# Half of the output-weight split moved behind attention, and the expert-pair sums moved from TensorE to GpSimd, in a one-core decoder layer

## What is computed

```
mix = concat(attn, pool, memo) @ w_o
h1  = layer_norm(alpha * x + mix)
f   = sum over the row's 2 experts e of gate_e * (silu(h1 @ w_gate[e]) * (h1 @ w_up[e])) @ w_down[e]
y   = layer_norm(alpha * h1 + f)
```

## Time and profile before

| | |
|---|---|
| median of 3 runs | 989.77 us (986.93 to 989.87) |
| the profiled execution | 986.13 us, span 984.3 us |
| PE busy | 898.5 us (91%) |
| DVE, ACT, POOL busy | 566.0, 388.0, 237.9 us |
| projections, attention | until about 213 us, until about 447 us |
| output projection and routing | from 450.7 us to about 596 us |
| experts | until about 937 us |
| tail | until 984.3 us |

### The profile page before, as it was taken

The page is one execution under the profiler, slowest core; times in us unless marked ns, Lnnn a source line. Parts: engine busy times, 40 slices in busy tenths (PEclk is TensorE's granted clock), DMA queues, the critical chain, the costliest instruction groups (busy, mean ns, idle before and its releaser), DMA issues.

```text
span 984.3 us, 13505 instructions
## 1 busy us (share of the span) xinstructions
PE 898.5 (91%) x5170; PEld 644.5 (65%) x5170; DVE 566.0 (58%) x1098; ACT 388.0 (39%) x741; POOL 237.9 (24%) x142
## 2 busy tenths in 40 slices
PE   6999999988999999868999986999999999999934
PEld 6999878964555544546878855666666666666511
DVE  6202021037665665574677684677787877777438
ACT  5202010014555655473110032454646464555226
POOL 0000000088100000051000003146555555555200
PEclk9999999998999999998999995999999999999968
DMA  9999999289876856606755536799999999997276
GB/s 354 311 345 369 350 362 369 83 328 259 299 291 245 296 172 234 206 37 263 247 183 212 194 130 214 259 346 362 362 352 362 348 361 368 363 370 283 83 293 252
DMA packets 54849, 273.50 MB, mean 278 GB/s; under 512 B 13984, under 2 KB 16544, under 8 KB 39680
## 3 DMA queue, kind: packets, MB, share of 16 engines
q1 hardware_dynamic: 46016, 247.97, 69.8%
q0 software_dynamic: 8768, 24.66, 7.1%
HBM read 256.33 MB, written 95.30 MB: 357 GB/s over the span
## 4 chain that ended last, share of the span: by engine, by line
PE 76%; DVE 14%; ACT 4%; issue 4%; DMA 2%; SPq 0%; DVEq 0%; POOLq 0%; ACTq 0%
PE psum L680 67%; PE psum L739 4%; PE psum L956 3%; ACT back L1065 1%; DVE stats L1387 1%; DVE back L1397 1%; DVE back L1393 1%; DVE back L1262 1%; DVE back L1384 1%; ACT back L512 1%; DMA middle<-pair_d 1%; PE psum L880 1%; DVE front L1270 1%; DVE front L1272 1%; DVE back L1238 1%
## 5 line engine op out<-in xcount | busy, mean ns | idle before, releaser
L1712 POOL DMA_INDIRECT pair_d<-front,back x32 | 134.4, 4199 | 161.4 <-DVE front L1515 155.6
L680 PE MATMUL psum<-back,front 128*64 128x128 f32 (+1 forms) x904 | 151.8, 361 | 5.5 <-ACT back L512 4.6
L680 PEld LDWEIGHTS psum<-back,front 128*64 128x64 f32 (+1 forms) x904 | 71.3, 148 | 61.4 <-issue 52.3
L680 PE MATMUL psum<-gu_high,xg_high 128*112 128x512 f32 x256 | 104.5, 408 | 2.1 <-DVE xg_low L1500 2.1
L680 PE MATMUL psum<-gu_high,xg_low 128*112 128x512 f32 x256 | 101.8, 398 | 0.0
L680 PE MATMUL psum<-gu_low,xg_high 128*112 128x512 f32 x256 | 101.7, 397 | 0.0
L680 PE MATMUL psum<-x_high,w_high 128*128 128x352 f32 x288 | 94.1, 327 | 8.3 <-DVE w_low L377 8.3
L680 PE MATMUL psum<-x_low,w_high 128*128 128x352 f32 x288 | 93.4, 324 | 0.0
L680 PE MATMUL psum<-x_high,w_low 128*128 128x352 f32 x288 | 93.2, 324 | 0.0
L1515 DVE SCALAR_TENSOR_TENSOR front<-psum,back 112x512 f32<-112x512 f32 x64 | 45.1, 747 | 68.8 <-PE psum L680 68.8
L680 PE MATMUL psum<-front 64*128 64x256 f32 (+5 forms) x320 | 79.9, 521 | 4.0 <-DVE stats L1238 2.7
(11 more groups left out here) (213 smaller groups left out, 1710.9 us busy)
## 6 DMA issues: line engine op xcount, KB each, us to landing
back<-w_gu SPq DMA_DIRECT2D x32, 1024.0 KB, 13.8
out_win_k_s<-cache_win_k SPq DMA_DIRECT2D x16, 2044.0 KB, 13.3
out_win_v_s<-cache_win_v SPq DMA_DIRECT2D x16, 2044.0 KB, 12.6
back<-w_down SPq DMA_DIRECT2D x25, 1024.0 KB, 13.0
front<-w_gu SPq DMA_DIRECT2D x16, 1024.0 KB, 13.0
middle<-w_gu SPq DMA_DIRECT2D x16, 1024.0 KB
back<-winkT SPq DMA_DIRECT2D x8, 1792.0 KB, 7.7
back<-cache_win_v SPq DMA_DIRECT2D x8, 1024.0 KB, 7.5
```

Source lines behind the costliest of these rows:

```text
L680: return nc.tensor.matmul(out, lhsT, rhs, start=start, stop=stop, skip_group_check=True)
L1712: G.indirect_dma_start(pair_d, bass.IndirectOffsetOnAxis(ap=IDX[0:CAP, NE + e:NE + e + 1], axis=0), YS[e % 2][0:CAP, :], None, bounds_chec ...
```

## The change

The split of the output weights keeps tiles 0 to 3 beside attention, now in units 40, 42, 44 and 46, with their low parts on GpSimd. Tiles 4 to 7 are split after attention: ACT's order is then `cat_high` of chunk 0, `wo_high` 4 to 7, `cat_high` of chunks 1 to 3; DVE's order is `cat_low` of chunk 0, `wo_low` 4 to 7, `cat_low` of chunks 1 to 3. PE waits at tiles 4 to 7 for a new semaphore `s_wor`. In the tail PE does nothing more: DVE sums chunks 0 and 1, both ahead of its first normalisation, and GpSimd sums chunks 2 to 8 in place in SBUF. The reads of all nine sums are now from SBUF.

```diff
-        OWN_SUM = (0, 1, 4, 8)
-        PE_SUM = [c for c in range(CH) if c not in OWN_SUM]
+        DVE_SUM = 2
         def row_sum(c):
-            if c in OWN_SUM:
-                return YP[c][:, 0, :]
-            j = PE_SUM.index(c)
-            return PS[:, 1024 * (j % 4):1024 * (j % 4) + 1024]
+            return YP[c][:, 0, :]
         def summed(eng, c):
-            if c in PE_SUM:
-                eng.wait_ge(s_ysum, PE_SUM.index(c) + 1)
+            if c < DVE_SUM:
+                eng.wait_ge(s_vsum, c + 1)
             else:
-                eng.wait_ge(s_vsum, OWN_SUM.index(c) + 1)
+                eng.wait_ge(s_ysum, c - DVE_SUM + 1)
...
-        WO_SPLIT_AT = {40: (0,), 41: (1,), 42: (2,), 43: (3,), 44: (4,), 45: (5,), 46: (6,), 47: (7,)}
+        WO_SPLIT_AT = {40: 0, 42: 1, 44: 2, 46: 3}
+        WO_EARLY = len(WO_SPLIT_AT)
...
# TensorE, the first chunk's products, and its sums in the tail
-                        pe.wait_ge(s_wol, k + 1)
+                        if k < WO_EARLY:
+                            pe.wait_ge(s_wol, k + 1)
+                        else:
+                            pe.wait_ge(s_wor, k - WO_EARLY + 1)
...
-            for j, c in enumerate(PE_SUM):
-                m = rows(c)
-                pe.wait_ge(s_yp[c], 16)
-                if j >= 4:
-                    pe.wait_ge(s_f1, PE_SUM[j - 4] + 1)
-                for n in range(2):
-                    o = row_sum(c)[0:m, 512 * n:512 * n + 512]
-                    mm(o, ident[0:m, 0:m], YP[c][0:m, 0, 512 * n:512 * n + 512], True, False)
-                    last = mm(o, ident[0:m, 0:m], YP[c][0:m, 1, 512 * n:512 * n + 512], False, True)
-                last.then_inc(s_ysum, 1)
...
# ScalarE, after the last unit
-            for c in range(4):
+            cat_rounded(0)
+            for k in range(WO_EARLY, KT):
+                wo_rounded(k)
+            for c in range(1, 4):
                 cat_rounded(c)
...
# VectorE, after the last unit
-            for c in range(4):
+            cat_rest(0)
+            for k in range(WO_EARLY, KT):
+                full, high, low = wo_parts(k)
+                dve.wait_ge(s_hi, len(splits) + 1 + k + 1)
+                V_.tensor_tensor(low, full, high.bitcast(F32), ALU.subtract).then_inc(s_wor, 1)
+            for c in range(1, 4):
                 cat_rest(c)
...
# VectorE, tail
-            own_sum(0)
+            for c in range(DVE_SUM):
+                own_sum(c)
             for c in range(CH):
-                if c + 1 in OWN_SUM:
-                    own_sum(c + 1)
                 normalised(c)
...
# GpSimd
-            for k in range(KT):
+            for k in range(WO_EARLY):
                 full, high, low = wo_parts(k)
...
+            for c in range(DVE_SUM, CH):
+                pool.wait_ge(s_yp[c], 16)
+                y = YP[c][0:rows(c)]
+                G.tensor_tensor(y[:, 0, :], y[:, 0, :], y[:, 1, :], ALU.add).then_inc(s_ysum, 1)
```

More of the change, by code:

```diff
@@ L248, in build @@
         s_xp, s_xe, s_sexp, s_smin, s_srd = sem("s_xp"), sem("s_xe"), sem("s_sexp"), sem("s_smin"), sem("s_srd")
-        s_dve, s_pl, s_qb, s_wol = (sem(n) for n in ("s_dve", "s_pl", "s_qb", "s_wol"))
+        s_dve, s_pl, s_qb, s_wol, s_wor = (sem(n) for n in ("s_dve", "s_pl", "s_qb", "s_wol", "s_wor"))
         s_wo = [sem(f"s_wo{i}") for i in range(2)]
@@ L1026, in _ @@
                 pe.nop()
-            pe.wait_ge(s_yd, 2 * NE)
-            for j, c in enumerate(PE_SUM):
-                m = rows(c)
-                pe.wait_ge(s_yp[c], 16)
-                if j >= 4:
-                    pe.wait_ge(s_f1, PE_SUM[j - 4] + 1)
-                for n in range(2):
-                    o = row_sum(c)[0:m, 512 * n:512 * n + 512]
-                    mm(o, ident[0:m, 0:m], YP[c][0:m, 0, 512 * n:512 * n + 512], True, False)
-                    last = mm(o, ident[0:m, 0:m], YP[c][0:m, 1, 512 * n:512 * n + 512], False, True)
-                last.then_inc(s_ysum, 1)
         @block.scalar
@@ L1085, in o_out, with wo_rounded @@
                 nc.scalar.copy(CAT[:, hp + (0 if kind == "w" else 6), i * P:i * P + P], bank(6 + u % 2)[:, 0:P]).then_inc(s_OB, 1)
+            def wo_rounded(k):
+                act.wait_ge(s_wo[k // 4], 16)
+                full, high, _ = wo_parts(k)
+                nc.scalar.copy(high, full).then_inc(s_hi, 1)
             exps(0, 0)
@@ L1103, in _ @@
                     x_act(e)
-                for k in WO_SPLIT_AT.get(u, ()):
-                    act.wait_ge(s_wo[k // 4], 16)
+                if u in WO_SPLIT_AT:
                     act.wait_ge(s_S, 2 * 32)
                     act.wait_ge(s_store, 16 * (6 + 2 * DB))
-                    full, high, _ = wo_parts(k)
-                    nc.scalar.copy(high, full).then_inc(s_hi, 1)
+                    wo_rounded(WO_SPLIT_AT[u])
             o_out(NU - 1)
@@ L1370, in cat_rest @@
                 full, high, low = cat_parts(c)
-                dve.wait_ge(s_hi, len(splits) + KT + c + 1)
+                dve.wait_ge(s_hi, len(splits) + (KT if c else WO_EARLY) + c + 1)
                 V_.tensor_tensor(low, full, high.bitcast(F32), ALU.subtract).then_inc(s_lo, 1)
-            for c in range(4):
+            cat_rest(0)
[4 more added lines that the diff above has]
+            for c in range(1, 4):
                 cat_rest(c)
```

## The result

| | before | after |
|---|---|---|
| median of 11 runs each | 988.71 us (985.93 to 989.87) | 990.88 us (990.43 to 993.24) |
| ratio of the runs | | 1.0031, 95% interval 1.002 to 1.0042 |
| the profiled execution, its span | 986.13, 984.3 us | 992.58, 990.8 us |
| PE, DVE, POOL busy | 898.5, 566.0, 237.9 us | 878.5, 581.0, 250.8 us |

Slower by 0.31%, 3.1 us by the ratio (the two medians are 2.2 us apart). The forecast was slower by 7.3 us, to 997.1, and its range began at 991.0.

A forecast was written before the change was run, and what follows sets the result against it. The prediction took DVE to bound the tail and the PE, DVE, PE chain the projection's start. -1.6 (weights) + 8.9 (sums) = +7.3 us on the median 989.77 gave 997.1, range 991 to 1000.5.

The forecast's parts named there:

- What bounds the tail, and what the change does to it: Tail: DVE bounds it at 2.72 us a chunk; GpSimd's seven sums and DVE's long instructions take turns, 8.9 us later.
- Rival 1: Tail: no turns, `scalar_tensor_tensor` doesn't wait for GpSimd, DVE ends at 976.4; 7.1 us faster, 982.7; chance 0.12.
- Rival 2: Tail: turns at half the price, t near 1.1 us; +0.6 us in all, 990.4; chance 0.06.
- The price of a turn: Tail: one GpSimd sum adds t = 2.2 us to DVE, seven of them 15.2 us of blocking.
- The tail that it was set against: Tail before: DVE ends at 981.93 and idles 3.60 us, because PE's sum of chunk 2 is late.
- The weight split: Start of the projection: PE's first product 1.6 us earlier (0.22 + 0.28 + 1.08), bounds 0.3 to 2.2 us.
- 0.22 us counted for attention: Attention: removed GpSimd instructions had slowed the divisions on DVE at 442.60, 0.84 against 0.62 us.
- three tiles take 3.3 us: Projection: PE's time for three weight tiles before tile 4, each further one 0.7 us, so it never waits.
- rival 3: Projection: PE waits for the late weight tiles, at most 4.8 us less the gain, 1001; chance 0.04.
- Rivals 3 and 4: Fourth rival, projection: the weight edit does nothing, the copy's chain sets the end; +8.9 - 0.3, 998.4, within the forecast's 0.78.
- The level: Whole kernel: the change of +7.3 us was put on the median of the runs, 989.77, giving 997.1.
- Rival 5: Start of the projection: the fall of PE's granted clock may come elsewhere; 1 us either way, within the forecast's 0.78.

The follow-up runs named there:

- e4: The changed kernel with DVE making all nine sums, one ahead of each normalisation, and GpSimd none: median 986.88 us, ratio 0.9995 to the kernel before.
- e6: The kernel of e1 with GpSimd also making the sums of chunks 2, 3, 5, 6 and 7, unread, into free SBUF: one run, span 986.4 us.
- e1: Only the weight split of the change, with the tail of the kernel before: median 985.87 us, ratio 0.9983 to the kernel before.
- e8: The kernel of e1 with only two weight tiles split beside attention, in units 44 and 46, and six behind it: median 983.96 us, ratio 0.9963.
- e3: The changed kernel unaltered, run again on the chip of e1: median 993.17 us, ratio 1.0057 to the kernel before.
- e2: Only the sums of the change, with the weight split of the kernel before: median 995.76 us, ratio 1.0077 to the kernel before.
- e9: The changed kernel unaltered, run once more on the chip of e11: median 992.95 us, ratio 1.0052 to the kernel before.
- e7: The kernel of e1 with 15 products of constants on PE between the last expert and its first sum: median 983.17 us, ratio 0.9952.
- e10: The kernel of e1 with GpSimd making one sum, chunk 2's, and PE those of 3, 5, 6 and 7: median 984.88 us, ratio 0.997.
- e5: The changed kernel with GpSimd doubling the first row in place instead of adding the second, one SBUF input: one run, span 981.7 us.
- e11: e7 and e8 together, two weight tiles beside attention and PE kept at work before the tail: median 984.13 us, ratio 0.9946.

## Why the prediction came out as it did

**What bounds the tail, and what the change does to it: right.** Seven DVE instructions, no more, were held, one by each GpSimd sum, in turn; ACT had its part ready each time; five chunks at 2.72 us followed. e4 and e6 leave no other cause: without GpSimd 1.28 us, with one operand in PSUM 1.28 us. The Trainium skill's rule (SBUF — State Buffer, § Who interferes with whom) held for `scalar_tensor_tensor`, which no row of before could show. Rivals 1 and 2 are out by the same rows. Rival 2's time, 990.4, is near the first measurement, but its price of 1.1 us a turn isn't what the rows show. Its sum is also 0.8 us too high: it adds the turns to 976.4, which holds idle time that turns would fill, and not to 951.1 + 24.5 = 975.6.

**The price of a turn: mis-sized, and this is the step that failed.** I took t = 2.2 us for what one GpSimd sum adds to DVE, from a single row in which DVE's instruction arrived when GpSimd's had been running for 1.1 us. Such a row shows how early the hold ends, 0.13 us before the record's end, but not how late it begins. In the full turns a held instruction is 3.18 to 3.25 us instead of 1.28, so t is 1.93. The hold ends 0.19 us before the sum does and begins about 0.15 us late, and the small rest is the reciprocal and the gap between instructions, which pass while the sum runs. Seven turns are 13.5 us, where the forecast had 15.2: 1.7 us too much. It is the whole difference between the 8.9 us forecast for the tail and the 7.2 in the pair of profiles. I had a lower bound of 1.65 for t, so the term was in its range, but I centred on the row's upper reading.

**The tail that it was set against: up to 1.1 us off, not settled.** I took DVE's 3.60 us of idle time for a constant. It hangs on PE's clock: in e1 and e8, whose tail is the same code, it was 4.76 and 4.94 us and the time from the last scatter to the end 47.5 us against 46.4 in the profile of before. With seven turns that time is 53.6 to 53.7 us, in all three profiles of the changed kernel. So by the profiles the loss is 6.1 to 7.2 us, and not 8.9. The medians speak for the upper end: e3 is 7.3 us above e1 on the same chip, and e2 is 7.6 us slower than before, each with 2 us or so of uncertainty.

**The weight split: right.** 1.6 us earlier was forecast, e1 measured 1.7 (0.5 to 2.9). `cat_low` at 1.22 us, no wait at tiles 4 to 7 and the gap (1.33 us shorter, where 0.28 + 1.08 = 1.36 had been worked out) all came. The 0.22 us counted for attention can't be told: from the first cast to PE's last attention product the new split takes 20.0 to 20.8 us and the old one 20.4 and 21.0. A slip in the working did no harm: "three tiles take 3.3 us" is the time of eight products, and nine take 3.56. Rivals 3 and 4 are out for this split; e8 shows rival 3 in small, 0.3 us, with six late tiles. That the casts of the even units are the costly ones was right too: taking out two of them brought 2.0 us. The forecast said that this cost stays, which is why the edit brought so little.

**The level: 1.1 us off.** I put the change on the median of three runs, 989.77. Eleven gave 988.71. Rival 5, the clock, is real but goes with the execution and not with the edit: chunk 0's 48 products took 12.7 to 13.8 us in the profiles in which PE didn't wait for a tile, 12.74 before and 12.91 after.

Together: 7.3 less 1.7 (turns) and up to 1.1 (tail) is 4.5 to 5.6 us. The repeats measured 5.6 and 5.1 (1.0057 and 1.0052), and the first measurement came out below (1.0031, 3.1 us). In absolute times, 997.1 less 1.7 and 1.1 (level) is 994.3, and 993.2 with the whole 1.1 of the tail; the medians of e3 and e9 are 993.17 and 992.95. The first series' 990.88 is 2 us below those, and what made it so isn't known. Within one kernel the upstream waits vary by as much (the first cast at 425.61, 426.08 and 427.73 us in the three profiles of the changed kernel), but a whole series at one level was not traced.

The range began at 991.0, 0.1 us above the measured 990.88. Its lower edge already took the lowest of the three runs together with the smallest price of a turn, 986.9 + 5. What it took off for the weight split was only 0.9 us, a number that the working doesn't explain: the forecast's own term is 1.6, its bound 2.2. With 1.6 the edge is 990.3. Such a miss or hit by 0.1 us says little; the forecast's centre was 4 us too high by the ratio of the first measurement and 2 us by those of the repeats, and the turns account for 1.7 of that.

## What to carry to other kernels

GpSimd is no free helper beside a DVE that is the bound: a two-input instruction on SBUF held the next DVE instruction with two SBUF operands for 1.93 us, while DVE would have done the same sum in 1.15. Either leave one operand of DVE's instruction in PSUM, as PE's sums did here, or let DVE do it. And before work is taken from PE because it is late, look at its granted clock: fifteen idle products brought 3.1 us against e1 (e7), and a single GpSimd sum in the same place 1.3, not clear of the noise (e10).

## What the runs showed of the hardware that was not expected

- A held pair costs less than the sum of its records: GpSimd 2.35 and DVE 1.28 alone, 3.29 a pair in turn, not 3.63.
- A one-input GpSimd instruction of the same width held one DVE instruction with two SBUF operands for 0.66 us and the next one, L1264 with two SBUF operands as well, not at all (e5, one run). The Trainium skill's rule (SBUF — State Buffer, § Who interferes with whom) names any GpSimd instruction that reads SBUF, whatever the number of its inputs, and calls the hold an exclusive lock. For this one-input instruction the measurement decides, and it says less.
- Kernels that are the same up to unit 40 reach it at 425.57 to 429.24 us (eleven profiles). That spread of 3.7 us above the edit is as large as the change's effect (3.1 to 5.6 us), so a single pair of profiles can't size it.
- PE's clock held over an idle gap of 2.1 us in e7 and fell over one of 2.15 in e11, with the same 15 products before it.
